# Attention units in pairs of heads: half-array matmuls in place of padded copies

## Chip, cores and metric

The kernel runs on one core of one Trainium2 chip. The metric is the device time of one execution in microseconds. The engines are named TensorE (PE), VectorE (DVE), ScalarE (ACT), GpSimd (POOL) and SyncE (SP).

## What is computed

Two layers of a hybrid decoder over 256 positions and a model width of 1024. Each layer projects the normalised input once (`w_in`), runs three groups of heads side by side, joins them by one output projection (`w_out`), and then a squared-ReLU MLP. The part that matters here is the attention of groups A and C:

```python
# group C: 8 heads of 64 in 2 kv groups of 4, three branches, gates by sigmoid
s_s = einsum('bqghd,bqgtd->bqght', qrb, ks) * scale      # selected blocks (here: all causal keys)
o_s = einsum('bqght,bqgtd->bqghd', softmax(s_s), vs)
s_w = einsum('bqghd,bsgd->bqghs', qrb, kw) * scale       # sliding window (here: all causal keys)
o_w = einsum('bqghs,bsgd->bqghd', softmax(s_w), vw)
o = gb[..., 0:1] * o_c + gb[..., 1:2] * o_s + gb[..., 2:3] * o_w
# group A: 4 heads of 64, keys limited to the top 64 of an indexer's scores
```

Group C's 16 score matrices (8 heads, 2 branches) and group A's 4 are 256x256, causal, fp32. The compressed branch `o_c`, the S5 group B with its GELU and gated unit, and the indexer's top-64 selection run in between.

## The kernel before

All engines run hand-written programs side by side, one per engine, each strictly in its written order, with semaphores (`Signal`: `x.by(instruction)` counts up, `wait_ge(x.sem, x.at(L, n))` waits). fp32 weights come as 92 pieces per layer through a ring of four `raw` buffers: SyncE loads (`piece`), ScalarE makes the high part (`hi`), VectorE or GpSimd the low part (`lo`, `lo_out`), TensorE multiplies three products (`mm3`). Plain fp32 matmuls (`mm`) show in the trace as two passes of load and matmul each.

A causal score matrix of one head is held as 384 columns: 128 queries by 128 keys, and 128 queries by 256 keys. The loop of a layer goes over 20 units, `units`: for each block `b` of heads (2b, 2b+1) of group C its head and branch, then the 4 heads of group A. The stages of unit `i`, by engine:

- TensorE: two score matmuls into bank `pb[i % 2]`, with zero-padded keys (`kT`, `akT`: 128 rows, 64 of them zero, by `mhalf`), after `s_sb` of unit i-2; then three transposes of unit i-3 (after `pn_sb`, banks `pb[2 + u % 2]`); then two value matmuls of unit i-4 (after `pT_sb`) with zero-padded values (`vpad`, `av`: 64 of 128 columns zero); then what `between` names.
- VectorE: after `s_ps`, two evacuations with scale, mask and row maximum (line 1437, `s_sb`); then for unit i-1, after `e_sb`, `reciprocal` and the gate's product (lines 1449, 1452, `cf_sb`); then `between`: rounds of `top8_of_rest`, group C's small works (`c_open1`, `c_gelu`, `c_keys`, `c_max`, `c_probs`), group B's (`y_cube`, `y_gelu`, `y_half`, `y_glu`), `a_mask`, and `h_rest`.
- ScalarE: after `s_sb`, two exponentials with row sums (lines 998, 1000, `e_sb`); then the copy of the transposes of unit i-3 out of PSUM (line 1007, `pT_sb`); then `transposed`, `hi` (pieces 20 to 23), tanh and copies for the other groups, at the end the splits of the outputs.
- GpSimd: after `cf_sb`, the products of exponentials and coefficients (line 748, `pn_sb`), and after units 3, 7, 11, 15 the low part of pieces 20 to 23 (line 738, `lo_out`).

Ahead of the loop TensorE does `s5_kernel`; in `between` it does `c_first` and `a_keys` behind unit 1, `a_queries` behind 4, `c_second` and `s5_out` behind 5 (these wait for ScalarE's copy of the queries, `transposed(7)`, in unit 5), `c_scores` behind 8, `c_transpose` and `y_turned` behind 13, `glu` and `c_values` behind 15. `y_turned` waits for eight transfers (`ytok`) that SyncE issues once VectorE's `y_gelu` is done. The loop ends with `sums_of`, and the output projection follows.

At the start VectorE sets `av` and `vpad` to zero (line 1196), between the low parts of pieces 3 and 4, while GpSimd runs `prep`; GpSimd's `rstd` behind it gates the first tile's copy.

## Time and profile before

| | |
|---|---|
| median of 3 runs | 733.24 us (731.89 to 733.95) |
| profiled execution | 735.1 us, span 733.1 us |
| mean granted clock | 0.967 |
| TensorE busy | 664.8 us (91%), weight loads 586.9 us |
| VectorE, ScalarE, GpSimd busy | 450.8, 367.1, 228.2 us |

The profile is of one execution. Its time stands 2.0 us above its span, and 1.9 us above the median of the other runs. Busy shares are averages over stages with different limits; the two attention loops, from 96 to 166 us and from 447 to 515 us, are under a fifth of the span. PEclk is the granted clock of TensorE, 1.00 for 2.4 GHz and 0.50 for 1.2 GHz.

### The profile page before, as it was taken

How to read it: one execution, taken by the hardware profiler on the slowest of the kernel's cores; microseconds unless marked ns; L12 is line 12 of the kernel's file. 1: busy time of each engine (PE TensorE's matmuls, PEld its weight loads, DVE VectorE, ACT ScalarE, POOL GpSimd, SP SyncE). 2: the span in 40 equal slices, each digit the busy share in tenths (PEclk: the TensorE clock that was granted, in tenths of full speed). 3: DMA queues.
4: the chain of work that ended last, by engine and by line, in shares of the span. 5: the costliest groups of instructions: out<-in, count | busy, mean ns of one | idle time of the engine just before them, and what ended most of it. 6: DMA issues, size and time to landing. Idle time of an engine off the chain costs nothing.

```text
span 733.1 us, 11482 instructions
## 1 busy us (share of the span) xinstructions
PE 664.8 (91%) x4308; PEld 586.9 (80%) x4308; DVE 450.8 (61%) x860; ACT 367.1 (50%) x680; POOL 228.2 (31%) x379
## 2 busy tenths in 40 slices
PE   5959878779899999999999987977989999999996
PEld 4847767568798899988978886756879889999884
DVE  8675974843755559596555659584375555455553
ACT  5542755563544543445545567556354444444542
POOL 5899433441034399980000001544100000000001
PEclk9988998998999999999999999999899999999998
DMA  9485020200685555637535722020065665666541
GB/s 267 125 220 149 30 41 30 73 30 29 202 237 201 170 186 169 225 119 247 168 119 164 228 79 41 30 73 30 29 202 178 196 188 171 208 182 198 177 140 57
DMA packets 62965, 102.77 MB, mean 140 GB/s; under 512 B 20677, under 2 KB 27022, under 8 KB 62878
## 3 DMA queue, kind: packets, MB, share of 16 engines
q1 hardware_dynamic: 58862, 98.63, 44.1%
q0 software_dynamic: 592, 1.70, 0.9%
q10 hardware_dynamic: 3456, 1.70, 0.9%
q8 instruction: 34, 0.56, 0.3%
q14 instruction: 21, 0.17, 0.1%
HBM read 99.66 MB, written 1.31 MB: 138 GB/s over the span
## 4 chain that ended last, share of the span: by engine, by line
PE 72%; DVE 14%; ACT 6%; issue 3%; DMA 2%; POOL 1%; SPq 0%; DVEq 0%; POOLq 0%; ACTq 0%
PE pb L1542 70%; DVE w_lo L1179 5%; DMA raw<-in_w_in 2%; DVE tab_zone L1437 2%; DVE x L1109 1%; ACT w_hi L804 1%; DVE dtmp L1102 1%; ACT tab_zone L1000 1%; PE pb L1675 1%; DVE h_lo L1109 1%; ACT ptmp L1007 1%; DVE cprob L1102 1%; PE pb L1825 1%; POOL sp L584 1%; ACT tab_zone L998 1%
## 5 line engine op out<-in xcount | busy, mean ns | idle before, releaser
L1179 DVE TENSOR_TENSOR w_lo<-raw,w_hi 128x1024 fp32r<-128x1024 f32 (+2 forms) x176 | 225.3, 1298 | 157.3 <-ACT w_hi L804 157.2
L804 ACT ACTIVATE w_hi<-raw 128x1024 fp32r<-128x1024 f32 (+2 forms) x184 | 187.7, 1026 | 224.4 <-PE pb L1542 200.4
L1542 PE MATMUL pb<-h_hi,w_hi 128*128 128x256 f32 x512 | 145.2, 284 | 2.5 <-DVE h_lo L1109 1.8
L1542 PE MATMUL pb<-h_hi,w_lo 128*128 128x256 f32 x512 | 144.9, 283 | 0.0
L1542 PE MATMUL pb<-h_lo,w_hi 128*128 128x256 f32 x512 | 144.9, 283 | 0.0
L1542 PEld LDWEIGHTS pb<-h_hi,w_hi 128*128 128x128 f32 x512 | 98.2, 192 | 4.1 <-DVE w_lo L1179 3.0
L1542 PE MATMUL pb<-w_hi,z_hi 128*128 128x512 f32 x256 | 99.9, 390 | 0.4 <-DVE w_lo L1179 0.4
L1542 PE MATMUL pb<-w_hi,z_lo 128*128 128x512 f32 x256 | 99.8, 390 | 0.0
L1542 PE MATMUL pb<-w_lo,z_hi 128*128 128x512 f32 x256 | 99.6, 389 | 0.0
L1542 PEld LDWEIGHTS pb<-h_hi,w_lo 128*128 128x128 f32 x512 | 98.2, 192 | 0.4
L1542 PE MATMUL pb<-w_hi,h_hi 128*128 128x512 f32 (+2 forms) x224 | 85.8, 383 | 13.9 <-DVE w_lo L1179 10.8
L1542 PEld LDWEIGHTS pb<-h_lo,w_hi 128*128 128x128 f32 x512 | 98.2, 192 | 0.0
L1542 PE MATMUL pb<-w_hi,h_lo 128*128 128x512 f32 (+2 forms) x224 | 83.8, 374 | 0.0
L1542 PE MATMUL pb<-w_lo,h_hi 128*128 128x512 f32 (+2 forms) x224 | 83.8, 374 | 0.0
L748 POOL TENSOR_TENSOR dtmp<-tab_zone,cf 128x128 f32<-128x128 f32 x80 | 40.7, 530 | 124.3 <-PE pb L1542 62.0
L1542 PEld LDWEIGHTS pb<-w_hi,h_hi 128*128 128x128 f32 x224 | 44.0, 196 | 22.2 <-issue 10.7
L1542 PEld LDWEIGHTS pb<-w_hi,z_hi 128*128 128x128 f32 x256 | 48.1, 188 | 10.5 <-DVE w_lo L1179 0.9
L1542 PEld LDWEIGHTS pb<-w_lo,z_hi 128*128 128x128 f32 x256 | 48.1, 188 | 10.1
L1542 PEld LDWEIGHTS pb<-w_hi,z_lo 128*128 128x128 f32 x256 | 48.1, 188 | 9.4
L584 POOL TENSOR_TENSOR tail<-tail 128x1 f32<-128x1 f32 x2 | 0.4, 193 | 177.2 <-ACT proj L1090 177.2
L1542 PEld LDWEIGHTS pb<-w_hi,h_lo 128*128 128x128 f32 x224 | 44.1, 197 | 6.5
L1542 PEld LDWEIGHTS pb<-w_lo,h_hi 128*128 128x128 f32 x224 | 43.6, 195 | 7.0
(304 smaller groups left out, 982.4 us busy)
## 6 DMA issues: line engine op xcount, KB each, us to landing
raw<-in_w_up SPq DMA_DIRECT2D x64, 512.0 KB, 3.7
raw<-in_w_down SPq DMA_DIRECT2D x64, 512.0 KB, 4.3
raw<-in_w_in SPq DMA_DIRECT2D x24, 512.0 KB, 4.7
raw<-in_w_out SPq DMA_DIRECT2D x16, 512.0 KB, 3.8
raw<-in_w_in SPq DMA_DIRECT2D x8, 308.0 KB, 3.5
raw<-in_w_in SPq DMA_DIRECT2D x8, 280.0 KB, 3.3
x<-in_x ACTq DMA_DIRECT2D x4, 256.0 KB, 4.2
u_zone<-proj SPq DMA_DIRECT2D x16, 32.0 KB, 2.1
```

The lines of the kernel that those rows point to most:

```text
L584: step(pool.tensor_tensor(o, a, b, op), wait)
L748: m = pool.tensor_tensor(pn[:, u % 3, a:b], ex[:, u % 3, a:b], cf[:, u % 2, t:t + 1].to_broadcast([PART, b - a]), ALU.mult)
L804: hi_made.by(act.activation(w_hi[:, n % RING, 0:width(n)], raw[:, n % RING, 0:width(n)], ACT.Copy))
L998: step(act.activation(ex[:, i % 3, 0:PART], sc[:, i % 2, 0:PART], ACT.Exp, scale=-1.0, bias=nmx[:, i % 2, 0:1], accum_out=sm[:, i % 3, 0:1 ...
L1000: e_sb.by(act.activation(ex[:, i % 3, PART:384], sc[:, i % 2, PART:384], ACT.Exp, scale=-1.0, bias=nmx[:, i % 2, 1:2], accum_out=sm[:, i % ...
L1007: pT_sb.by(act.activation(pT[:, u % 2, :], pb[2 + u % 2][:, 0:384], ACT.Copy))
L1102: step(dve.tensor_tensor(o, a, b, op), wait)
L1109: return dve.scalar_tensor_tensor(out=o, in0=a, scalar=s, in1=b, op0=op0, op1=op1)
L1179: lo_made.by(dve.tensor_tensor(w_lo[:, n % RING, 0:width(n)], raw[:, n % RING, 0:width(n)], w_hi[:, n % RING, 0:width(n)].bitcast(F32), AL ...
L1437: m = dve.tensor_tensor_reduce(sc[:, i % 2, a:b], pb[i % 2][:, a:b], mask[:, a:b], -(HD ** -0.5), 3e38, ALU.add, ALU.min, nmx[:, i % 2, t: ...
L1542: return pe.matmul(o, l, r, start=start, stop=stop, skip_group_check=True)
L1675: m = pe.transpose(pb[QK_BANK[i]][:, b * SEQ + t * PART:b * SEQ + (t + 1) * PART], src[:, t], ident[:])
```

## The change

The unit of the loop becomes a pair: two heads of one branch. For group C these are head j of kv group 0 and head j of kv group 1 (before, heads 2b and 2b+1 of the same group), since their queries lie on rows 0 to 63 and 64 to 127 of one tile. Scores use row halves of the array (keys unpadded, one half each), the two heads in banks `pb[0]` and `pb[1]`; value products use column halves of the array, with `proj` and a smaller `av` read as they are. `vpad`, its copies, the masks on the key copies and two memsets go. Group C's output now comes in the order (j, g), so its gains and the rows of `w_out` are loaded in that order, by two DMAs in place of one for `gain_c` and for four pieces a layer. There are 10 pairs a layer, each stage handles both heads under one semaphore, the banks for the scores are not doubled any more (the next scores wait for `s_sb` of the pair before), transposes are two pairs behind and values three, and `between` is laid out anew on each engine.

```diff
+TWO_LOADS = (P_IN + 1, P_IN + 2, P_IN + 4, P_IN + 5)
+def landed(n):
+
+    return 16 * sum(2 if i in TWO_LOADS else 1 for i in range(n % RING, n + 1, RING))
...
-        akT = a_zone[:, 0:4 * SEQ].rearrange("p (a t) -> p a t", a=4)
+        akT = a_zone[:, 0:2 * SEQ].rearrange("p (a t) -> p a t", a=2)
...
-        kT = u_zone[:, 4 * SEQ:8 * SEQ].rearrange("p (b g t) -> p b g t", b=2, g=C_KV)
+        kT = u_zone[:, 4 * SEQ:6 * SEQ].rearrange("p (b t) -> p b t", b=2)
...
-        av = sb("av", [PART, TT, A_HEADS, PART])
-        vpad = sb("vpad", [PART, TT, 2, C_KV, 192])
+        av = sb("av", [PART, TT, A_HEADS, HD])
...
-        UNITS = 2 * C_HEADS + A_HEADS
+        UNITS = C_HEADS + A_HEADS // 2
...
-        units = []
-        for b in range(4):
-            for h in (2 * b, 2 * b + 1):
-                for br in range(2):
-                    units.append(("C", h, br, b))
-        for h in range(A_HEADS):
-            units.append(("A", h, 0, h // 2))
+        pairs = [("C", br, b) for b in range(4) for br in range(2)] + [("A", 0, b) for b in range(2)]
+        C_PAIRS = C_HEADS
...
+            for g in range(C_KV):
+                sp.dma_start(vrow_b[4:8, :, HD * g:HD * g + HD],
+                             gain_c.rearrange("l (g j d) -> g j l d", g=C_KV, d=HD)[g]).then_inc(rows_b.sem, 16)
+            for r, src in ((0, gain_a), (2, gain_b), (8, kv_norm_g), (9, s5_glu_b)):
...
+                        dst = raw[:, n % RING, :].rearrange("p (k n) -> p k n", k=2)
+                        if q < 2:
+                            piece(n, dst, wo_l[:, 2 * q:2 * q + 2, half * 512:half * 512 + 512])
+                        else:
+                            for g in range(C_KV):
+                                piece(n, dst[HD * g:HD * g + HD], wo_c[:, g, 2 * q - 4:2 * q - 2, half * 512:half * 512 + 512])
...
+                for p in range(UNITS):
+                    pool.wait_ge(cf_sb.sem, cf_sb.at(L, p + 1))
+                    if p >= 2:
+                        pool.wait_ge(pT_ps.sem, pT_ps.at(L, p - 1))
+                    for m in range(2):
+                        i = 2 * (p % 2) + m
+                        for t, (a, b) in enumerate(((0, PART), (PART, 384))):
+                            w = pool.tensor_tensor(pn[:, i, a:b], ex[:, i, a:b],
+                                                   cf[:, i, t:t + 1].to_broadcast([PART, b - a]), ALU.mult)
+                            if (m, t) != (1, 1):
+                                step(w, False)
+                    pn_sb.by(w)
+                    if p in (1, 3, 5, 7):
+                        lo_out(20 + p // 2)
...
+                for p in range(UNITS + 2):
+                    if p < UNITS:
+                        act.wait_ge(s_sb.sem, s_sb.at(L, p + 1))
+                        if p >= 2:
+                            act.wait_ge(pn_sb.sem, pn_sb.at(L, p - 1))
+                        for m in range(2):
+                            i = 2 * (p % 2) + m
+                            for t, (a, b) in enumerate(((0, PART), (PART, 384))):
+                                w = act.activation(ex[:, i, a:b], sc[:, i, a:b], ACT.Exp, scale=-1.0,
+                                                   bias=nmx[:, i, t:t + 1], accum_out=sm[:, i, t:t + 1])
+                                if (m, t) != (1, 1):
+                                    step(w, False)
+                        e_sb.by(w)
+                    if p >= 2:
+                        v = p - 2
+                        act.wait_ge(pT_ps.sem, pT_ps.at(L, v + 1))
+                        if v >= 2:
+                            act.wait_ge(pv_done.sem, pv_done.at(L, v - 1))
+                        for m in range(2):
+                            w = act.activation(pT[:, 2 * (v % 2) + m, :], pb[2 + m][:, 0:384], ACT.Copy)
+                            if m == 0:
+                                step(w, False)
+                        pT_sb.by(w)
+                    if p in (1, 2):
+                        transposed(6 + p - 1)
+                    if p in (1, 2, 4, 6):
+                        hi(L, 20 + (1, 2, 4, 6).index(p))
+                    if p == 1:
+                        act.wait_ge(tanh_in.sem, tanh_in.at(L, 1))
+                        tanh_c.by(act.activation(gt[:, 2, :], gt[:, 1, :], ACT.Tanh, scale=GELU_A))
+                    if p == 3:
                         act.wait_ge(y_ps.sem, y_ps.at(L, 1))
                         y_sq.by(act.activation(yt, pb[7][:], ACT.Square, scale=0.044715 ** 0.5))
+                    if p == 4:
                         act.wait_ge(y_in.sem, y_in.at(L, 1))
                         y_th.by(act.activation(y2, y2, ACT.Tanh, scale=GELU_A))
+                    if p == 5:
+                        act.wait_ge(cs_max.sem, cs_max.at(L, 1))
+                        cs_exp.by(act.activation(pc2[:], pc2[:], ACT.Exp))
+                    if p == 7:
                         act.wait_ge(yk_ps.sem, yk_ps.at(L, 1))
                         yk_sb.by(act.activation(yg, pb[7][:], ACT.Copy))
+                        act.wait_ge(pcT_ps.sem, pcT_ps.at(L, 1))
+                        pcT_sb.by(act.activation(pcT[:], pb[4][:, 0:SEQ], ACT.Copy))
...
+                    if p == 9:
...
+                    if p == 10:
+                        act.wait_ge(pv_done.sem, pv_done.at(L, C_PAIRS))
...
-                    for t in (av, vpad):
-                        step(dve.memset(t[:], 0.0), False)
...
+                    by_block = [cs[:, i, :].rearrange("p (t j g) -> p t j g", t=TT, g=2) for i in (1, 2)]
+                    tt(by_block[0], by_block[1], gate[:].rearrange("p t (g j n) -> p n t j g", g=2, n=3)[:, 0], ALU.mult)
                     tt(p2, p2, cs[:, 1, :].unsqueeze(2).to_broadcast([PART, 16, 16]), ALU.mult)
-                    for t in range(TT):
-                        m = dve.tensor_tensor(pc[:, t].rearrange("p (g j) n -> p j g n", g=2),
-                                              pc2[:, t].rearrange("p (j g) n -> p j g n", g=2),
-                                              cone[:, t, :].unsqueeze(1).unsqueeze(1).to_broadcast([PART, 4, 2, 16]), ALU.mult)
-                        if t == 0:
-                            step(m, False)
-                    pc_made.by(m)
+                    pc_made.by(dve.tensor_tensor(pc, pc2, cone[:].unsqueeze(2).to_broadcast([PART, TT, C_HEADS, 16]),
+                                                 ALU.mult))
...
+                top = top8_of_rest
+                between = {0: (top, top), 1: (c_open1, top), 2: (c_gelu, top), 3: (top, y_cube, c_keys),
+                           4: (top, y_gelu), 5: (c_max, top), 6: (c_probs, top), 7: (a_mask, y_half), 8: (y_glu,),
+                           9: (lambda: h_rest(8, gm[:, L], out_rows, K_ORDER, 0, 4),),
+                           10: (lambda: h_rest(8, gm[:, L], out_rows, K_ORDER, 4, 2),)}
+                assert sum(w.count(top) for w in between.values()) * 8 == TOPK
+                for p in range(UNITS + 1):
+                    if p < UNITS:
+                        mask = cmask if pairs[p][0] == "C" else abias
+                        dve.wait_ge(s_ps.sem, s_ps.at(L, p + 1))
+                        if p >= 2:
+                            dve.wait_ge(e_sb.sem, e_sb.at(L, p - 1))
                         dve.nop(nofuse=True)
+                        for m in range(2):
+                            i = 2 * (p % 2) + m
+                            for t, (a, b) in enumerate(((0, PART), (PART, 384))):
+                                w = dve.tensor_tensor_reduce(sc[:, i, a:b], pb[m][:, a:b], mask[:, a:b],
+                                                             -(HD ** -0.5), 3e38, ALU.add, ALU.min,
+                                                             nmx[:, i, t:t + 1])
+                                if (m, t) != (1, 1):
+                                    step(w, False)
+                        s_sb.by(w)
+                    if p >= 1:
+                        v = p - 1
+                        kind, br, b = pairs[v]
+                        both = slice(2 * (v % 2), 2 * (v % 2) + 2)
+                        dve.wait_ge(e_sb.sem, e_sb.at(L, v + 1))
+                        if v >= 2:
+                            dve.wait_ge(pn_sb.sem, pn_sb.at(L, v - 1))
+                        w = dve.reciprocal(cf[:, both], sm[:, both])
                         if kind == "C":
+                            step(w)
+                            w = dve.tensor_tensor(cf[:, both], cf[:, both], gate[:].rearrange("p t (g j n) -> p n j g t", g=2, n=3)
+                                                  [:, 1 + br, b], ALU.mult)
+                        cf_sb.by(w)
...
+                between = {0: (c_first, a_keys), 1: (a_queries,), 2: (c_second, s5_out), 4: (c_scores,),
+                           6: (y_turned,), 7: (c_transpose, glu), 8: (c_values,)}
+                for p in range(UNITS + 3):
+                    if p < UNITS:
+                        kind, br, b = pairs[p]
+                        if p >= 1:
+                            pe.wait_ge(s_sb.sem, s_sb.at(L, p))
+                        q, k = (cqrT[:, b], kT[:, br]) if kind == "C" else (aqT[:, b], akT[:, b])
+                        for t, (a, n) in enumerate(((0, PART), (PART, SEQ))):
+                            for m in range(2):
+                                d = slice(HD * m, HD * m + HD)
+                                w = mm(pb[m][:, a:a + n], q[d, t * PART:(t + 1) * PART], k[d, 0:n], t == 0, True)
+                        s_ps.by(w)
+                    if 2 <= p < UNITS + 2:
+                        v = p - 2
+                        pe.wait_ge(pn_sb.sem, pn_sb.at(L, v + 1))
+                        if v >= 1:
+                            pe.wait_ge(pT_sb.sem, pT_sb.at(L, v))
+                        for m in range(2):
+                            for c in range(3):
+                                w = pe.transpose(pb[2 + m][:, c * PART:(c + 1) * PART],
+                                                 pn[:, 2 * (v % 2) + m, c * PART:(c + 1) * PART], ident[:])
+                        pT_ps.by(w)
+                    if p >= 3:
+                        v = p - 3
+                        kind, br, b = pairs[v]
+                        pe.wait_ge(pT_sb.sem, pT_sb.at(L, v + 1))
                         if kind == "C":
                             o = pb[5 + b // 2][:, (b % 2) * SEQ:(b % 2 + 1) * SEQ]
+                            col = (O_VS, O_VW)[br]
+                            vs = [[proj[:, t, col + HD * m:col + HD * m + HD] for m in range(2)] for t in range(TT)]
                         else:
                             o = pb[4][:, b * SEQ:(b + 1) * SEQ]
+                            vs = [[av[:, t, 2 * b + m, :] for m in range(2)] for t in range(TT)]
+                        last = (kind == "A" or b > 2) and br == (kind == "C")
+                        for t in range(TT):
+                            for m in range(2):
+                                w = mm(o[HD * m:HD * m + HD, t * PART:SEQ], vs[t][m],
+                                       pT[:, 2 * (v % 2) + m, t * SEQ:SEQ + t * PART],
+                                       t == 0 and v in (0, C_PAIRS // 2, C_PAIRS), t == 1 and last)
+                        pv_done.by(w)
```

The `between` of before, for comparison: on VectorE `{0: top8, 1: top8, 2: c_open1, 3: top8, 4: c_gelu, 5: top8, 6: top8, 7: (y_cube, c_keys), 9: (y_gelu, c_max, top8), 10: top8, 11: top8, 12: c_probs, 13: a_mask, 15: y_half, 17: y_glu, 19: h_rest, 20: h_rest}`, counted in units, of which two make a pair.

## Rows read from the trace of the kernel before

**Rows 1.** The page of the profile: span, and the chain that ended last by engine.

```profile
span 733.1 us, 11482 instructions
...
PE 72%; DVE 14%; ACT 6%; issue 3%; DMA 2%; POOL 1%; SPq 0%; DVEq 0%; POOLq 0%; ACTq 0%
```

**Rows 2.** Windows, the loops of both layers: busy us (instructions) by engine, granted clock, DMA.

```profile
core 0: us, PE busy (x) PEld busy (x) DVE busy (x) ACT busy (x) POOL busy (x), PEclk, DMA share, GB/s
...
96.00:166.40 70.40, 56.17 (x422) 48.16 (x423) 42.14 (x202) 39.39 (x127) 29.57 (x44) 0.90 0.17 45
...
447.00:514.60 67.60, 54.20 (x423) 46.00 (x423) 42.44 (x202) 39.38 (x127) 29.57 (x44) 0.92 0.18 47
```

**Rows 3.** Timeline, layer 0, unit 11: start us, us, engine, line, instruction.

```profile
133.21 0.28 DVE L1437 CUSTOM_DVE_ANT_0 tab_zone<-pb,cmask 128x128 f32<-128x128 f32 x1
...
133.76 0.16 DVE L1449 RECIPROCAL cf<-sm 128x2 f32<-128x2 f32 x1
...
133.88 0.40 ACT L998 ACTIVATE tab_zone<-tab_zone,nmx 128x128 f32<-128x128 f32 x1 [0.85 <-DVE nmx L1437]
...
134.03 0.62 DVE L1330 MAX8 top<-dtmp 128x8 f32<-128x128 f32 x2
...
134.19 0.97 POOL L748 TENSOR_TENSOR dtmp<-tab_zone,cf 128x128 f32<-128x128 f32 x2 [1.24 <-DVE cf L1452]
...
134.77 0.47 ACT L1007 ACTIVATE ptmp<-pb 128x384 f32<-128x384 f32 x1
...
135.42 0.28 DVE L1437 CUSTOM_DVE_ANT_0 tab_zone<-pb,cmask 128x128 f32<-128x128 f32 x1
```

**Rows 4.** Timeline, layer 0, `y_cube` and the scores after `c_keys`.

```profile
122.08 0.68 DVE L1109 SCALAR_TENSOR_TENSOR yz<-yz,pb 128x512 f32<-128x512 f32 x1
...
123.37 0.28 DVE L1437 CUSTOM_DVE_ANT_0 tab_zone<-pb,cmask 128x128 f32<-128x128 f32 x1
```

**Rows 5.** Timeline, TensorE: scores of one unit, the last sums, and column quarters in layer 1.

```profile
125.77 0.53 PEld L1542 LDWEIGHTS pb<-u_zone 128*128 128x128 f32 x4
...
126.87 0.29 DVE L1437 CUSTOM_DVE_ANT_0 tab_zone<-pb,cmask 128x128 f32<-128x128 f32 x1 [2.59 <-PE pb L1542]
...
166.36 2.98 PEld L1542 LDWEIGHTS pb<-inv,proj 128*128 128x128 f32 x24
...
464.23 1.93 PE L1542 MATMUL pb<-ca,ez 128*32 128x128 f32 x64
...
466.09 0.92 PE L1542 MATMUL pb<-u_zone 128*128 128x128 f32 x4
```

**Rows 6.** Timeline, TensorE: `c_first`, `c_second` and the scores behind `s5_out`, both layers.

```profile
96.07 3.92 PE L1542 MATMUL pb<-dtmp,w 128*64 128x32 f32 x64 [0.85 <-DVE dtmp L1319]
...
112.95 0.38 PE L1542 MATMUL pb<-gk,w2d 64*128 64x32 f32 x2 [1.46 <-ACT w_zone L948]
...
117.93 0.52 PEld L1542 LDWEIGHTS pb<-u_zone 128*128 128x128 f32 x4 [0.20 <-issue]
...
462.78 0.38 PE L1542 MATMUL pb<-gk,w2d 64*128 64x32 f32 x2 [0.92 <-ACT w_zone L948]
...
514.62 2.96 PE L1542 MATMUL pb<-inv,proj 128*128 128x1 f32 x24
```

**Rows 7.** Windows: the end of `s5_out` in layer 0 (columns as in rows 2).

```profile
114.50:117.50 3.00, 3.00 (x64) 3.00 (x60) 0.00 (x0) 0.00 (x0) 0.00 (x0) 0.50 0.02 5
```

**Rows 8.** Timeline, layer 0: `y_glu` on VectorE beside the low part on GpSimd.

```profile
152.60 2.35 POOL L738 TENSOR_TENSOR w_lo<-raw,w_hi 128x1024 fp32r<-128x1024 f32 x1
...
153.54 1.96 DVE L1109 SCALAR_TENSOR_TENSOR dtmp<-yz 128x512 f32<-128x512 f32 x1 [0.51 <-ACT yz L1027]
```

**Rows 9.** Timeline: SyncE's queue, the issues of the S5 output's turn.

```profile
128.41 5.91 SPq L538 DMA_DIRECT2D ytok<-uu  x8
```

**Rows 10.** Timeline, start of the kernel: GpSimd's `prep`, VectorE's memset and low part.

```profile
19.52 2.18 POOL L584 TENSOR_TENSOR sp<-sp,vcol 128x8 f32<-128x8 f32 x2
...
19.65 1.34 DVE L1196 MEMSET vpad<- 128x1536 f32 x1 [0.27 <-issue]
...
20.91 0.74 DVE L1179 TENSOR_TENSOR w_lo<-raw,w_hi 128x616 fp32r<-128x616 f32 x1
```

More of the change, by code:

```diff
@@ L948, in transposed @@
                         m = act.activation(aqT.rearrange("p a b -> p (a b)"), src[:], ACT.Copy)
-                    else:
-                        for g in range(2):
-                            dst = kT[:, :, g, :] if what == 5 else akT[:, g::2, :]
-                            m = act.activation(dst, src[:].rearrange("p (b n) -> p b n", b=2), ACT.Copy,
-                                               scale=mhalf[:, g:g + 1])
-                            if g == 0:
-                                step(m, False)
+                    elif what == 5:
+                        m = act.activation(kT.rearrange("p b t -> p (b t)"), src[:], ACT.Copy)
+                    else:
+                        m = act.activation(akT.rearrange("p a b -> p (a b)"), src[:], ACT.Copy)
                     qk_sb.by(m)
@@ L1025, in _ @@
+                    if p == 8:
                         act.wait_ge(glu_ps.sem, glu_ps.at(L, 1))
@@ L1419, in _ @@
                 s5_lags()
-                between = {0: (top8_of_rest,), 1: (top8_of_rest,), 2: (c_open1,), 3: (top8_of_rest,),
-                           4: (c_gelu,), 5: (top8_of_rest,), 6: (top8_of_rest,), 7: (y_cube, c_keys),
-                           9: (y_gelu, c_max, top8_of_rest), 10: (top8_of_rest,), 11: (top8_of_rest,),
-                           12: (c_probs,), 13: (a_mask,), 15: (y_half,), 17: (y_glu,),
-                           19: (lambda: h_rest(8, gm[:, L], out_rows, K_ORDER, 0, 4),),
-                           UNITS: (lambda: h_rest(8, gm[:, L], out_rows, K_ORDER, 4, 2),)}
@@ L1807, in c_values @@
                     c_open.by(m)
-                between = {1: (c_first, a_keys), 4: (a_queries,), 5: (c_second, s5_out), 8: (c_scores,),
-                           13: (c_transpose, y_turned), 15: (glu, c_values)}
-                for i in range(UNITS + 4):
-                    if i < UNITS:
-                        kind, h, br, _ = units[i]
-                        if i >= 2:
-                            pe.wait_ge(s_sb.sem, s_sb.at(L, i - 1))
-                        q, k = (cqrT[:, h % 4, :], kT[:, br, h // 4, :]) if kind == "C" else (aqT[:, h // 2, :], akT[:, h, :])
-                        mm(pb[i % 2][:, 0:PART], q[:, 0:PART], k[:, 0:PART], True, True)
-                        s_ps.by(mm(pb[i % 2][:, PART:384], q[:, PART:SEQ], k[:, 0:SEQ], False, True))
-                    if 3 <= i < UNITS + 3:
-                        u = i - 3
-                        pe.wait_ge(pn_sb.sem, pn_sb.at(L, u + 1))
-                        if u >= 2:
-                            pe.wait_ge(pT_sb.sem, pT_sb.at(L, u - 1))
-                        for c in range(3):
-                            m = pe.transpose(pb[2 + u % 2][:, c * PART:(c + 1) * PART],
-                                             pn[:, u % 3, c * PART:(c + 1) * PART], ident[:])
-                        pT_ps.by(m)
-                    if i >= 4:
-                        u = i - 4
-                        kind, h, br, b = units[u]
-                        pe.wait_ge(pT_sb.sem, pT_sb.at(L, u + 1))
@@ L1840, in _ @@
-                        mm(o, vs[0], pT[:, u % 2, 0:SEQ], u in (0, C_HEADS, 2 * C_HEADS), False)
-                        pv_done.by(mm(o[:, PART:SEQ], vs[1], pT[:, u % 2, SEQ:384], False,
-                                      (kind == "A" or b > 2) and h % 2 == 1 and br == (kind == "C")))
-                    for work in between.get(i, ()):
+                            vs = [[av[:, t, 2 * b + m, :] for m in range(2)] for t in range(TT)]
+                        last = (kind == "A" or b > 2) and br == (kind == "C")
@@ L1844, in _ @@
+                        for t in range(TT):
[4 more added lines that the diff above has]
+                        pv_done.by(w)
+                    for work in between.get(p, ()):
                         work()
```

121 lines of the change are left out of this document (18 added, 103 removed).

## The prediction, made before the result

> **What bounds the kernel now.** I read four views. The page says that TensorE ends the chain for 72% of the 733.1 us span [rows 1], which invites "fewer TensorE passes, less time". The windows over the two attention loops, 70.4 and 67.6 us, show otherwise there: no engine is busy throughout, TensorE 56 and 54 us, VectorE 42, ScalarE 39, GpSimd 30 [rows 2]. The loops are bound by turns that go round the engines. The timeline gives the price of one turn, and the rows around `c_first`, `c_second` and `s5_out` show where TensorE itself stands and waits for one.
>
> In steady state a unit goes: scores, 1.10 us from the first weight load to VectorE's start [rows 5]; then 0.67 to the first exponential and 0.89 to the copy of the transposes (133.21, 133.88, 134.77) [rows 3]. I call scores-evacuation, exponential and copy a turn. For one unit it takes 0.67 + 0.89 + 0.4 = 1.95 us. Behind the loop TensorE is dense again, so a shift of the loop's end shifts the end of the kernel.
>
> **Prices of a pair.** ScalarE and VectorE do the same instructions on the same shapes, two units in a row, and the semaphore comes after the second. Evacuation: 0.67 plus another 0.55 (133.21 to 133.76) = 1.22. Exponentials 2 x 0.89 = 1.78. Copies 0.8. A turn H is 3.8 us in place of 1.95. VectorE's own stream is 1.1 + 0.28 = 1.38 a pair (133.21 to 134.03 is 0.82 for a unit, of which 0.27 now falls once for two), and a round of top-8 is 1.39 (134.03 to 135.42). GpSimd's products are 2 x 0.97 = 1.94 [rows 3].
>
> Scores S on row halves: no row shows two row halves at once. Below, it costs what one unit does, 1.10; above, serial, 1.10 + 0.65 (the second unit's passes) = 1.75. Column quarters do overlap at fp32: 64 passes of 128 columns take 1.93 us, 30 ns each, and the full-array scores start at once behind them (466.09 against 464.23 + 1.93) [rows 5], so I charge 0.1 us for a change of tiling. But a load of 128 columns cannot shrink: 24 of them with one-column matmuls take 2.98 us, 124 ns each [rows 5]. A pair needs eight, 0.95 us, then the last pass and the latency: S = 1.5. Values have 64-column loads and overlap by column: 0.65 a pair; six transposes 0.65.
>
> The Trainium skill is on both sides here. TensorEngine Tiling (Array Packing), section Theoretical Speedup, gives up to twofold when the contraction is at most 64; by that S would be near 1.10 and is the second rival. TensorE: Matmul & The Clock Gate, section LDWEIGHTS, says a load's time follows its columns, not its rows; by that S stays near 1.5. The load rows bear out the second.
>
> **One layer, turn by turn.** The places where TensorE or VectorE waits for a turn in the new order, each with the work that it then does. The small works between pairs are read like `y_cube` and `c_keys`, 1.29 us (122.08 to 123.37) [rows 4]: `c_open1` 1.45, `c_gelu` 0.7, `c_max` 1.3, `c_probs` 2.2 among GpSimd's products.
>
> To `c_second`: `c_first` 3.9 and `a_keys` 0.3 stay in front [rows 6]. Then S 1.5, evacuation and `c_open1` and `a_queries` 3.25, S 1.5, H and the copy of queries 4.4: 14.85 us. Before it was 112.95 - 96.07 = 16.9 in layer 0 and about 15.7 in layer 1 [rows 2, 6]. The gain is 2.0 and 0.8.
>
> `s5_out` and its start: 117.93 - 112.95 = 5.0 in layer 0, where the granted clock fell to 0.50 [rows 6, 7], and 3.3 in layer 1 (462.78 to 466.09), at full clock [rows 5, 6]. In the new order TensorE idles some 4 us just before, as it did before the low stretch; I take 4.6 in both: gain 0.4, loss 1.3.
>
> From the scores behind `s5_out` to the last sums, in order: S 1.5; pair 3, H + square 0.6 + `y_cube`, `c_keys` 1.3 = 5.7; pair 4, H + high part 0.95 + tanh 0.65 + `y_gelu` 0.6 = 6.0, because `y_gelu` now stands in the same iteration as its tanh and VectorE waits; pair 5, 1.38 + `c_max` + top-8 = 4.1; pair 6, 1.38 + `c_probs` + top-8 = 5.0, and 0.7 more, since `y_turned` now comes before the scores of pair 7 and its eight transfers take 5.9 us to issue from `y_gelu` on [rows 9], some 2 to land, then turn and S; pair 7, H + 0.6 + `glu` 2.4 (1.7 at full clock, 3.4 at half) + S = 8.3; pair 8, `y_glu` is ready after H + 0.8 but GpSimd's `w_lo` lies beside it as before, when a 0.7 us instruction took 1.96 until `w_lo` was over [rows 8]: 6.5. Pair 9 and the tail: H, the splits with `h_rest` 3.7, which delay the last coefficients, GpSimd 0.25 + 1.94, then transposes, copies and values 2.35, and 0.85 for the half clock in part of it, as at the end before: 12.9. Sum 50.7, against 166.36 - 117.93 = 48.4 in layer 0 and the same 48.4 in layer 1.
>
> A layer is 14.85 + 4.6 + 50.7 = 70.15: against 70.3 in layer 0 and 67.5 in layer 1, -0.15 and +2.65.
>
> **Outside the loop.** The memsets of `av` and `vpad` go. In layer 0, `w_lo` waits behind the second one, 19.65 to 20.99, and GpSimd's `prep`, which later gates the first tile's copy, gets on only when `w_lo` is done: 2.18 us for two tiny products [rows 10]. Without the memset `w_lo` ends about 1.25 us sooner: gain 1.2. ScalarE's masked key copies, `vpad` and half of the `av` copies go before the loop, some 2 us, but `c_first` waits for VectorE's `cx` and hides it: nothing. If that cover were gone it would be 0.6. `akT` in one copy saves 0.6 in pair 1, off the path. SyncE issues one DMA more for `gain_c` ahead of the fifth piece, hidden by tile 0 on TensorE, and four pieces of `w_out` as two DMAs each; those are in flight during the loop, long before their use, and SyncE waits there for `lo_made` anyway. Its only late follower would be the `ytok` issues, already counted. `c_probs` in two instructions fewer: in the 2.2.
>
> Sum: -0.15 + 2.65 - 1.2 = +1.3 us. The profiled execution took 735.1 (span 733.1), so it becomes 736.4; the median of the three runs shown, 733.24, becomes 734.6. A difference within 0.3% (2.2 us) is not told from no change.
>
> **Rivals.** First, about even, my forecast: TensorE's savings fall where it waits, and doubled turns cost what fewer turns save. 734.6, chance 0.38; its own range 731 to 735.5.
>
> Second, faster: S comes down to 1.10, as one unit, five times on the path (pairs 1, 2, 3, 7, 8): 2.0 us a layer; with the clock full over `s5_out` a further 1.3. From 734.6 that is 4.0 to 6.6 off: 728 to 730.6. For it: column quarters reach full overlap [rows 5]. Against: the loads. It decides from S below about 1.2. Chance 0.26, including any gain over 2.2 us.
>
> Third, slower, and one mechanism: TensorE's clock. It was at half for 3.0 us of `s5_out` [rows 7] and 0.90 and 0.92 over the loops [rows 2]. Turns of 5 to 8 us with 2.3 us of TensorE work a pair leave it idler than units did. With half clock in all five scores on the path (loads and passes twice as long, +1.2 each where it meets them, say three of five), `glu` (+1.0) and the tail (+0.8) a layer loses 5.4 at most and 2 to 3 as a mean: 738.6 to 740.6; the border of 2.2 us is crossed with half a microsecond more a layer than I charged. For it: each low stretch stands behind an idle one. Chance 0.33 with its lesser forms.
>
> Fourth, the halves don't overlap at all, and the change gives only its regrouping: S = 1.75, five times in two layers +2.5: 737.1. Chance 0.03. The Trainium skill, TensorEngine Tiling (Array Packing), section Key Properties, has each change of tiling mode drain the engine, which speaks against three changes a pair; the scores that start as the column quarters end [rows 5] show no such price, so its sum would be the forecast's with 0.1 us of S already charged.
>
> Slower thus has 0.36, faster 0.26, same 0.38. The range reaches from clock full everywhere with S at 1.3 (-5) to S serial with some more half clock (+5.5): 729.5 to 740.
>
> **What would show it.** In the new profile: the step from the scores' first load to VectorE 1.5 us; 1.2 and 1.8 to exponential and copy; `c_second` 14.9 us after `c_first`; VectorE idle about 2.5 us before `y_gelu`; TensorE waiting for `ytok`'s transfers before pair 7; TensorE busy some 10 us less a loop while the loops stay near 70 us; GpSimd's `prep` 1.2 us sooner. I am wrong if VectorE or ScalarE streams without these stops, so that a loop takes 60 us, or if low clock stretches make it 74.

## The result, and the profile after

The changed kernel takes 745.06 us, median of 4 runs (742.62 to 751.44), beside 733.6 for the kernel before on the same chip: ratio 1.016, 95% interval 1.0112 to 1.0208, clear of no change. It is slower by 11.5 us, outside the range of the prediction (729.5 to 740); the forecast of 734.6 was wrong. The profiled execution took 744.2 (span 742.1), against 735.1 (733.1). The page, its span and its chain [rows 1]:

```profile
span 742.1 us, 11323 instructions
...
PE 63%; DVE 16%; issue 7%; POOL 5%; ACT 4%; DMA 3%; SPq 2%; DVEq 0%; POOLq 0%; ACTq 0%
```

TensorE has lost share of the chain, VectorE and GpSimd have gained it. Windows over the same two stretches as before, first pass of `c_first` to the last sums [rows 2]:

```profile
core 0: us, PE busy (x) PEld busy (x) DVE busy (x) ACT busy (x) POOL busy (x), PEclk, DMA share, GB/s
94.70:169.00 74.30, 52.03 (x422) 37.82 (x422) 38.87 (x182) 37.85 (x126) 29.23 (x44) 0.75 0.18 43
449.70:523.50 73.80, 54.63 (x422) 39.80 (x422) 38.89 (x181) 37.84 (x126) 29.20 (x44) 0.72 0.18 43
```

The loops take 74.3 and 73.8 us, where they took 70.4 and 67.6. VectorE has 3 us less work, TensorE 4 less in layer 0 and as much as before in layer 1, though the padded half of its score and value products is gone: the granted clock has fallen from 0.90 and 0.92 to 0.75 and 0.72. TensorE's instructions in time order, the places of [rows 6]:

```profile
94.75 5.43 PE L1545 MATMUL pb<-dtmp,w 128*64 128x32 f32 x64 [1.85 <-DVE dtmp L1327]
100.12 1.12 PE L1678 MATMUL pb<-ident,ak 128*128 128x128 f32 x4
101.17 1.65 PE L1545 MATMUL pb<-u_zone 64*128 64x128 f32 x8
106.07 1.12 PE L1678 MATMUL pb<-ident,proj 128*128 128x128 f32 x4 [3.25 <-DVE gt L1377]
107.11 1.65 PE L1545 MATMUL pb<-u_zone 64*128 64x128 f32 x8
...
113.42 0.38 PE L1545 MATMUL pb<-gk,w2d 64*128 64x32 f32 x2 [3.18 <-ACT w_zone L959]
...
118.34 0.93 PE L1545 MATMUL pb<-u_zone 64*128 64x128 f32 x8
...
169.00 2.84 PE L1545 MATMUL pb<-inv,proj 128*128 128x1 f32 x24
```
```profile
449.70 5.40 PE L1545 MATMUL pb<-dtmp,w 128*64 128x32 f32 x64 [1.37 <-DVE dtmp L1327]
...
468.33 0.38 PE L1545 MATMUL pb<-gk,w2d 64*128 64x32 f32 x2 [3.18 <-ACT w_zone L959]
...
523.53 2.84 PE L1545 MATMUL pb<-inv,proj 128*128 128x1 f32 x24
```

So the 9.0 us of span fall like this. `c_first` starts 1.3 sooner (94.75, was 96.07). The loop of layer 0 takes 74.25 from `c_first` to the sums, was 70.40: +3.85. From there to `c_first` of layer 1, 280.70, was 280.63: nothing. The loop of layer 1 takes 73.83, was 67.52: +6.3. The rest, 218.6, was 218.5. The same 64 matmuls of `c_first` took 3.92 us before, now 5.43 and 5.40; `c_second` follows it by 18.7 us in both layers, was 16.9 and 15.7. The clock over these pieces of layer 0, the idle stretch before `c_first` first (columns as in the windows above):

```profile
92.90:94.75 1.85, 0.01 (x2) 0.00 (x0) 1.85 (x8) 0.00 (x0) 0.00 (x0) 1.00 0.00 0
94.75:101.17 6.42, 6.42 (x69) 6.02 (x69) 4.48 (x24) 1.86 (x8) 0.00 (x0) 0.65 0.23 63
101.17:113.42 12.25, 5.83 (x28) 3.75 (x27) 8.21 (x40) 6.67 (x23) 4.80 (x9) 0.62 0.22 28
113.42:118.34 4.92, 4.92 (x100) 4.38 (x100) 0.00 (x0) 0.80 (x1) 1.38 (x1) 0.65 0.38 102
118.34:169.00 50.66, 34.87 (x232) 23.67 (x228) 26.14 (x117) 28.52 (x95) 23.05 (x35) 0.80 0.14 38
```

A pair at full clock, with all engines, reads as follows (the row that answers to [rows 3] and the scores of [rows 5]):

```profile
118.34 0.52 PEld L1545 LDWEIGHTS pb<-u_zone 64*128 64x128 f32 x8 [0.20 <-issue]
118.34 0.93 PE L1545 MATMUL pb<-u_zone 64*128 64x128 f32 x8
...
119.45 0.29 DVE L1438 CUSTOM_DVE_ANT_0 sc_zone<-pb,cmask 128x128 f32<-128x128 f32 x1 [6.92 <-PE pb L1545]
...
120.69 0.40 ACT L1004 ACTIVATE tab_zone<-sc_zone,nmx 128x128 f32<-128x128 f32 x1 [6.47 <-DVE nmx L1438]
...
121.02 1.90 POOL L759 TENSOR_TENSOR dtmp<-tab_zone,cf 128x128 f32<-128x128 f32 x4 [6.22 <-DVE cf L1454]
...
122.46 0.84 ACT L1015 ACTIVATE ptmp<-pb 128x384 f32<-128x384 f32 x2
```

The scores of a pair reach VectorE 1.11 us after their first load, the exponentials begin 1.24 later, the copies 1.77 after that. The later pairs, with `y_cube`, `y_gelu` and the turn of `ytok` [rows 4, 9]:

```profile
123.81 0.69 DVE L1119 SCALAR_TENSOR_TENSOR yz<-yz,pb 128x512 f32<-128x512 f32 x1 [1.48 <-ACT yz L1028]
...
125.11 0.28 DVE L1438 CUSTOM_DVE_ANT_0 sc_zone<-pb,cmask 128x128 f32<-128x128 f32 x1
...
130.45 0.69 DVE L1119 SCALAR_TENSOR_TENSOR uu<-yz,pb 128x512 f32<-128x512 f32 x1 [2.47 <-ACT yz L1031]
130.93 1.63 SPq L503 DMA_DIRECT2D raw<-in_w_out  x2
...
132.60 5.11 SPq L547 DMA_DIRECT2D ytok<-uu  x8
...
139.22 1.11 PE L1770 MATMUL pb<-ident,ytok 128*128 128x128 f32 x4 [1.19 <-DMA ytok<-uu]
...
142.10 0.29 DVE L1438 CUSTOM_DVE_ANT_0 sc_zone<-pb,cmask 128x128 f32<-128x128 f32 x1 [1.64 <-PE pb L1545]
```

And the start: the low part that began at 20.91 behind the memset of `vpad` [rows 10] now begins at 19.42:

```profile
19.42 1.61 DVE L1189 TENSOR_TENSOR w_lo<-raw,w_hi 128x616 fp32r<-128x616 f32 x2 [1.12 <-ACT w_hi L815]
```

### The profile page after: what moved, and what is told of

Read it like the earlier page. It is cut to its first block, busy times and chain, and to the rows that moved or that the text cites. A ratio compares the mean times of both kernels' runs of the same rounds, so it can differ in the third digit from the quotient of the medians.

```text
span 742.1 us, 11323 instructions
## 1 busy us (share of the span) xinstructions
PE 657.5 (89%) x4308; PEld 567.2 (76%) x4308; DVE 443.1 (60%) x818; ACT 361.3 (49%) x668; POOL 226.1 (30%) x379
## 4 chain that ended last, share of the span: by engine, by line
PE 63%; DVE 16%; issue 7%; POOL 5%; ACT 4%; DMA 3%; SPq 2%; DVEq 0%; POOLq 0%; ACTq 0%
PE pb L1545 62%; DVE w_lo L1189 5%; POOL dtmp L759 2%; DVE dtmp L1112 2%; DMA raw<-in_w_in 2%; DVE x L1119 1%; POOL w_lo L747 1%; ACT tab_zone L1004 1%; SPq L547 1%; DVE sc_zone L1438 1%; ACT w_hi L815 1%; DVE h_lo L1119 1%; DVE cn L1287 1%; DVE dtmp L1327 1%; DMA ytok<-uu 1%
## 5 line engine op out<-in xcount | busy, mean ns | idle before, releaser
L1004 ACT ACTIVATE tab_zone<-sc_zone,nmx 128x128 f32<-128x128 f32 x80 | 35.4, 443 | 69.8 <-DVE nmx L1438 69.8
```

Source lines behind the costliest of these rows:

```text
L1004: w = act.activation(ex[:, i, a:b], sc[:, i, a:b], ACT.Exp, scale=-1.0, bias=nmx[:, i, t:t + 1], accum_out=sm[:, i, t:t + 1])
```

## Experiments

Two theories were set against each other. A: TensorE's clock made the loss; the pieces of the forecast hold at full clock. B: the pairs' turns cost more than charged, and the clock only follows. All times are medians, the ratio is to the kernel before on the same chip, with its 95% interval. That neighbour took 733.6 us beside the changed kernel, 734.4 beside e1 to e4, 734.0 beside e5 to e8 and 734.1 beside e10 to e13; what a run gains or loses is told against its own neighbour.

| kernel | us | ratio | span, clock of the profile |
|---|---|---|---|
| changed | 745.1 | 1.016 (1.0112 to 1.0208) | 742.1, 0.931 |
| e1 changed, filled at the start | 738.1 | 1.0055 (1.0028 to 1.0082) | 736.2, 0.946 |
| e2 changed, filled | 732.6 | 0.9972 (0.9946 to 0.9998) | 730.0, 0.981 |
| e3 before, filled | 727.3 | 0.9902 (0.9864 to 0.994) | 725.5, 0.981 |
| e4 pairs, whole array | 750.7 | 1.0229 (1.0183 to 1.0274) | 751.4, 0.948 |
| e5 single heads, half forms | 754.7 | 1.0274 (1.0239 to 1.031) | 755.8, 0.925 |
| e6 changed, ytok first | 745.6 | 1.015 (1.0123 to 1.0177) | 745.3, 0.926 |
| e7 before, memsets first | 732.6 | 0.9985 (0.9958 to 1.0011) | 730.5, 0.969 |
| e8 changed, filled (7 more in the tail), ytok first | 734.4 | 0.9994 (0.9969 to 1.0018) | 729.2, 0.983 |
| e10 single heads, half scores | 741.6 | 1.0108 (1.0083 to 1.0133) | 740.4, 0.946 |
| e11 single heads, half values | 735.1 | 1.0018 (0.9994 to 1.0041) | 735.4, 0.967 |
| e12 pairs, whole array, filled as e8 | 740.2 | 1.0083 (1.0052 to 1.0114) | 735.3, 0.986 |
| e13 before, filled, memsets moved | 724.9 | 0.9892 (0.9866 to 0.9918) | 726.9, 0.983 |

**Filling the waits (e1, e2, e3).** The filling is work that nobody reads, whole-array matmuls of the identity into a bank that is free at that place:

```diff
+            def fill(n, bank=6):
+                for _ in range(n):
+                    mm(pb[bank][:, 384:512], ident[:], ident[:], True, True)
...
                 def c_first():
-                    pe.wait_ge(cx_made.sem, cx_made.at(L, 1))
                     pe.wait_ge(qk_sb.sem, qk_sb.at(L, 5))
+                    fill(8)
+                    pe.wait_ge(cx_made.sem, cx_made.at(L, 1))
...
                 def a_queries():
+                    fill(14)
...
                 def c_second():
+                    fill(14)
```

> The changed kernel with 36 more matmuls a layer of the identity by itself (128 columns, nobody reads them), put where TensorE waits at the start of the loop: 8 before c_first, 14 before the queries' transposes, 14 before c_second. Theory A (the clock made the loss: c_first took 5.4 us instead of 3.9 and the stretch to c_second 18.7 instead of the 14.9 forecast, because TensorE had stood idle and its clock then fell to half): c_first is back at about 3.9, c_second comes 15.0 to 16.0 us after it, each layer loses 3 us, 738 to 740 us. Theory B (the doubled turns themselves make the stretch long, the clock only follows): the granted clock rises but c_second stays 18 us behind c_first and the time stays at 744 to 746.

e2 adds 6, 6, 6 and 4 before the transposes of iterations 4 to 7, 5 after iteration 5, 5 before `y_turned`, and 18 and 10 before the transposes of iterations 10 and 11 (bank 4).

> The same and further such matmuls in the long waits of the later pairs, before the value products of the tail too: the clock should be full nearly everywhere in the loop and over the first passes of the output projection. Theory A: both loops near 66 to 68 us and the time 730 to 734, level with the kernel before or under it. Theory B: both loops stay over 72 us and the time 742 to 747, since the filling can only stand in the way.

e3 does the same in the kernel before, at the five places that its expectation names, 40 matmuls a layer.

> Control: the kernel before, whose own loops had granted clocks of 0.90 and 0.92, with the same kind of filling in its four longest waits a layer (4 matmuls before c_first, 10 before the first value product, 6 before c_second, 9 before the turn of the block probabilities, 11 in the tail). Theory A: it has low stretches of its own to lose, about 1.5 us a layer at s5_out and 1 in the tail, 728 to 731. Theory B: no change, 733 to 734. If the filled change of the run beside it ends above this one, the change loses by its turns as well as by the clock.

TensorE's rows of e1 in both layers, then windows over the loops of e2 and of e3:

```profile
94.54 3.92 PE L1545 MATMUL pb<-dtmp,w 128*64 128x32 f32 x64
...
109.58 0.38 PE L1545 MATMUL pb<-gk,w2d 64*128 64x32 f32 x2 [0.99 <-ACT w_zone L959]
```
```profile
446.75 3.92 PE L1545 MATMUL pb<-dtmp,w 128*64 128x32 f32 x64
...
461.80 0.38 PE L1545 MATMUL pb<-gk,w2d 64*128 64x32 f32 x2 [0.99 <-ACT w_zone L959]
```
```profile
94.00:161.60 67.60, 60.43 (x598) 49.33 (x598) 38.72 (x181) 37.84 (x126) 29.23 (x44) 1.00 0.19 47
444.75:511.47 66.72, 60.44 (x600) 49.33 (x599) 38.21 (x179) 37.84 (x126) 29.25 (x44) 1.00 0.18 48
```
```profile
95.87:161.00 65.13, 59.16 (x495) 51.67 (x495) 42.77 (x201) 39.17 (x127) 29.61 (x44) 0.97 0.19 49
441.90:507.10 65.20, 59.42 (x497) 51.85 (x496) 42.13 (x197) 39.17 (x127) 29.60 (x44) 0.97 0.18 49
```

Theory A holds for the larger part: with 36 filling matmuls a layer the changed kernel loses 3.7 us to the kernel before, where it lost 11.5. `c_first` is back at 3.92, `c_second` comes 15.04 us behind it in both layers (forecast 14.85). In e2 the clock is full throughout the loops, they are 67.6 and 66.7 us, and the kernel gains 1.8. The control gains too, 7.1 us, and its loops are 65.1 and 65.2. So of the 11.5 us, 5.3 remain when both are filled (732.6 against 727.3 on one chip), and the other 6.2 go with the clock: B holds for the 5.3. In the spans, 730.0 and 725.5, that is +2.5 and +1.5 in the loops, 1.9 less before `c_first`, and 2.2 behind the first loop, where e2's output projection begins at half clock (in e3 the granted clock is 1.00 from 160 to 176):

```profile
150.00:162.00 12.00, 10.15 (x89) 8.46 (x88) 3.45 (x14) 8.45 (x27) 3.80 (x8) 1.00 0.12 44
162.00:172.00 10.00, 10.00 (x46) 8.77 (x47) 2.27 (x4) 1.97 (x7) 1.49 (x4) 0.66 0.01 2
```

**Half forms or pairs (e4, e5, e10, e11, e12).** e4 keeps the order of pairs and widens the products; e5 keeps single heads and narrows them, on the padded copies that the kernel before makes anyway; e10 and e11 are the two halves of e5's edit. e4 and e12 leave out the padding as well, so that each head of a pair gets the sum of both heads' products: they stand for the time of whole-array passes only.

```diff
 e4:
-                                w = mm(pb[m][:, a:a + n], q[d, t * PART:(t + 1) * PART], k[d, 0:n], t == 0, True)
+                                w = mm(pb[m][:, a:a + n], q[:, t * PART:(t + 1) * PART], k[:, 0:n], t == 0, True)
 ...
 e5, e10 (d: the head's 64 rows):
-                        mm(pb[i % 2][:, 0:PART], q[:, 0:PART], k[:, 0:PART], True, True)
+                        mm(pb[i % 2][:, 0:PART], q[d, 0:PART], k[d, 0:PART], True, True)
 ...
 e5, e11:
-                            vs = [vpad[:, t, br, h // 4, a:a + PART] for t in range(TT)]
+                            vs = [vpad[:, t, br, h // 4, HD:PART] for t in range(TT)]
 ...
```

> The changed kernel in its order of pairs, but every score and value product over the whole array, as the padded copies had it (here without the padding, so each head of a pair gets the sum of both heads' scores and value products; the time of the passes is that of padded ones). Per pair the scores cost about 0.7 us more and the values 0.8 more at full clock. If the half-array forms are what leaves TensorE too thinly used and lets the clock fall: c_first back at 3.9, loops' clock back at 0.90, and the time 739 to 744 in spite of the longer passes. If the regrouping into pairs does it: c_first stays at 5.4, the clock stays near 0.75 and the longer scores come on top, 748 to 752.

> The kernel before, one head at a time and with its padded copies still made, but its score products read only the 64 rows of the head and its value products only the 64 columns: the half-array forms without pairs, so nothing overlaps. If the half forms by themselves lower the granted clock: the loops fall from 0.90 and 0.92 to about 0.75, c_first takes over 5 us, and the time is 738 to 742. If they cost nothing and the pairs' longer turns are the cause: the loops stay at 68 to 70 us and the time at 732 to 735.

`c_first` of e4 in both layers, then of e5 (with the loads of one unit's scores), and of e10 in layer 0:

```profile
94.80 5.94 PE L1545 MATMUL pb<-dtmp,w 128*64 128x32 f32 x64 [1.47 <-DVE dtmp L1327]
...
455.52 5.04 PE L1545 MATMUL pb<-dtmp,w 128*64 128x32 f32 x64 [0.72 <-DVE dtmp L1327]
```
```profile
97.09 3.92 PE L1542 MATMUL pb<-dtmp,w 128*64 128x32 f32 x64 [0.30 <-DVE dtmp L1319]
...
120.96 0.52 PEld L1542 LDWEIGHTS pb<-u_zone 64*128 64x128 f32 x4 [0.20 <-issue]
```
```profile
96.44 6.02 PE L1542 MATMUL pb<-dtmp,w 128*64 128x32 f32 x64 [0.76 <-DVE dtmp L1319]
```

e4 took 5.94 us for it after 1.47 us idle, with whole-array scores ahead; e5 took 3.92 behind half-array scores, with 0.30 us idle. So half-array scores are not needed for the loss here: the regrouping brings it by itself. The length of the wait does not decide it alone either. In layer 1 of e4 the same passes took 5.04 us behind a wait of 0.72, and in layer 0 of e10, single heads with scores on 64 rows, 6.02 behind 0.76, while the kernel before took 3.92 behind 0.85 [rows 6]. What does show is that filling in front of `c_first` brings the 3.92 back (e1). And e5 is the slowest kernel of all, 754.7 us, outside both of its forecasts, though its `c_first` ran at full clock. Its windows, and a stretch of the kernel before in which most of the same units run:

```profile
121.00:131.00 10.00, 10.00 (x62) 6.83 (x59) 5.72 (x32) 6.03 (x18) 5.22 (x7) 0.99 0.01 2
131.00:156.60 25.60, 25.60 (x76) 14.53 (x74) 16.31 (x71) 11.52 (x39) 9.55 (x15) 0.50 0.19 53
```
```profile
119.67:140.00 20.33, 15.02 (x95) 12.34 (x93) 16.90 (x76) 12.71 (x40) 11.44 (x16) 1.00 0.15 41
```

In e5 the clock fell to half while TensorE was busy for 25.6 of 25.6 us, and it had been busy all of the 10 us ahead. The kernel before stood idle for a quarter of the time and kept the full clock over these 20.3 us. My first reading, a low stretch stands behind an idle one, is half the story: half-array passes did it without an idle moment. The Trainium skill, TensorE: Matmul & The Clock Gate, section What's actually happening, lets the clock go by how busy TensorE has been; by that rule alone this stretch would be at full clock, and the measurement decides otherwise. What the chip counts instead stays open here.

> The kernel before in single heads with only the score products cut to the head's 64 rows (values stay over the whole array). With both forms cut it took 754.7 us, and TensorE's clock was at half for 26 us a layer while TensorE was busy throughout (136 to 156: 20.0 of 20.0 us busy, clock 0.50). If the clock follows how much of the array works and row halves alone suffice: low stretches of over 10 us a layer, 742 to 752. If both forms have to come together: 733 to 736, loops at 0.88 to 0.92.

> The same with only the value products cut to 64 columns (scores whole). If column halves lower the clock as row halves do: 740 to 750. If only rows matter, the columns being the narrower part of the work anyway: 733 to 736.

Row halves cost 7.6 us by themselves, column halves nothing that this run separates from no change (interval 0.9994 to 1.0041). Both together cost 20.7, far more than the sum: at half clock TensorE itself becomes what the loop waits for (the 25.6 us above). Why the two together hold the clock down so long is not shown. The loops of e10:

```profile
96.40:171.10 74.70, 67.80 (x422) 52.80 (x423) 42.16 (x201) 39.22 (x127) 29.61 (x44) 0.77 0.18 43
450.30:521.90 71.60, 63.11 (x422) 49.51 (x423) 42.02 (x201) 39.32 (x127) 29.64 (x44) 0.83 0.18 44
```

> The changed kernel in pairs with score and value products over the whole array (each head of a pair gets the sum of both, as in the fourth run) and the filling of the eighth. If, once the clock is held up, half forms are worth what their passes save (0.65 us a pair for scores, 0.65 for values where they are on the path, some 5 places a layer): 736 to 741, against 732 to 734 for the filled change. If they are worth nothing at full clock because the turns of the other engines set the pace: 731 to 734.

```profile
95.40:166.20 70.80, 67.63 (x613) 63.96 (x613) 38.54 (x180) 37.87 (x126) 29.28 (x44) 1.00 0.18 45
448.40:518.50 70.10, 67.58 (x614) 63.93 (x614) 37.84 (x175) 37.87 (x126) 29.30 (x44) 1.00 0.17 45
```

At full clock pairs over the whole array take 70.8 and 70.1 us a loop, pairs in halves 67.6 and 66.7, single heads over the whole array (e3, clock 0.97) 65.1 and 65.2. The half forms give 3.3 us a layer, the regrouping costs 5.3. In kernel time the half forms give 5.7 us between e12 and e8, which have the same filling. What inside the regrouping costs the 5.3, the turns of double length, the banks for the scores that are no longer doubled, or the new layout of `between`, no run separates. As the kernels run, unfilled, the regrouping costs 16 us (e4) and the half forms give back some 5 in pairs, while in single heads, where nothing overlaps, they cost 20.7.

**The queue and the memsets (e6, e7, e8).** e6 changes one line, `if n == 26:` to `if n == 25:` in front of the eight `ytok` issues; e8 makes that change in e2 and raises the filling of iteration 11 from 10 to 17; e7 moves the two memsets to VectorE's first instructions.

> The changed kernel with one line moved: SyncE issues the eight ytok transfers before the piece of w_out that is now two transfers, not behind it. ytok's issues begin about 0.8 to 1.6 us sooner and y_turned stops waiting (it waited 1.2 us in layer 0 and 2.8 in layer 1). If that queue is on the path: 742 to 743.5. If VectorE's probabilities and top-8 would have held pair 7 back anyway: no change, 744 to 745.5.

> The kernel before with its two memsets of the padded copies moved to VectorE's first instructions, nothing else: the only part of the change that I booked as a gain outside the loop. If the memset behind which w_lo and with it GpSimd's preparation waited is what brought c_first 1.3 us forward (94.75 against 96.07): c_first at about 94.8 and 732 to 732.7. If the shorter copies of ScalarE brought it: c_first stays at 96.1 and the time at 733.6.

> The changed kernel with the filling of the second run, 7 more of those matmuls behind the value products of pair 7 in the tail (there TensorE had idled 1.5 us and the output projection's first passes ran at half clock, 163 to 170), and ytok's transfers first. If clock and queue explain what is left but the turns: 2 us for the clock and 1 to 2 for the queue, 728.5 to 730.5. The filled kernel before took 727.3; what stays above that is the price of the doubled turns. If the turns of pairs are the larger part: 731 to 733.

e6 in order of time, `y_gelu` on VectorE, the issues, the turn on TensorE:

```profile
132.16 0.69 DVE L1119 SCALAR_TENSOR_TENSOR uu<-yz,pb 128x512 f32<-128x512 f32 x1 [2.47 <-ACT yz L1031]
...
132.88 5.50 SPq L547 DMA_DIRECT2D ytok<-uu  x8
...
140.71 0.65 PE L1770 MATMUL pb<-ident,ytok 128*128 128x128 f32 x4 [0.97 <-DMA ytok<-uu]
```

SyncE takes the issues up 0.03 us after the end of `y_gelu` (132.85), where it took 1.46 (131.14 to 132.60). VectorE's start on pair 7 comes 5.53 us after that on pair 6 (136.88 to 142.41), was 6.94, in layer 1 5.82, was 6.04; before it VectorE now waits 0.23 and 0.51 us, so the rest is its own work. So the queue was on the path, by 1.4 and 0.2 us, and the kernel's time shows nothing of it (ratio 1.015, was 1.016): the scores behind `s5_out`, which the edit can't touch, reach VectorE at 121.16 instead of 119.45 in this execution. Half clock for a little longer or shorter is worth as much as the queue; that this is what hid it is my reading, not shown. e8, at 734.4 above both of its forecasts, is not better than e2 either (729.5 to 736.5 against 729.3 to 736.1), though in its profiled execution the clock behind the first loop is 0.95 (162 to 166) and 0.75 (166 to 172), where e2 has 0.68 and 0.65. e7: TensorE's next wait for a low part ended 20.85 us after its first pass, was 22.19; but that first pass came 0.9 later (13.46, was 12.59), since the memsets now stood ahead of it; `c_first` at 95.91, was 96.07. The time decides nothing (interval 0.9958 to 1.0011).

**The best kernel (e13).** e3 with nine more filling matmuls, and the memsets behind the low parts of pieces 16 and 17:

```diff
                 for n in range(12, 20):
                     lo(n)
+                    if L == 0 and n in (16, 17):
+                        step(dve.memset((av, vpad)[n - 16][:], 0.0), False)
```

> The filled kernel before (727.3) with 9 more filling matmuls before the value product of the eighth unit, where its clock still fell (128 to 134), and the two memsets of the padded copies moved behind the low parts of pieces 16 and 17, where VectorE waits 1.9 us a piece. If the memset's place is worth the 1.3 us by which the gate of the second tile moved: 724.5 to 726. If moving them only shifts the wait, as the kernel with the memsets first gave 0.5 us: 726.5 to 727.5.

It beats both kernels, 1.1% under the one before (median 724.9; the profiled execution took 729.0). That it beats e3 is not shown (their intervals overlap). The first passes of tile 1 came 1.3 us sooner (55.18, was 56.48), but `cx` only 0.5 (its memset at 93.30, was 93.80): between the two VectorE waited for ScalarE's copies.

## Why the prediction was wrong, point by point

**The step that failed** is the sum of a layer, 14.85 + 4.6 + 50.7 = 70.15, and what it was set against. I made it at full clock but for 0.85 us in the tail, put the clock's further cost at nothing, and left it to the third rival with 0.33 and "2 to 3 as a mean" a layer. Filling turns a loss of 11.5 us into a gain of 1.8, 13.3 us; the kernel before had 7.1 of the same to lose, so by the clock the change added 6.2, or 3.1 a layer. That is close to the rival's own price: the mechanism was named and roughly sized, and booked at nothing. The other 5.3 us are there with both kernels filled, where I had +1.3 in all. I had put the clock's cost in scores, `glu` and the tail; it began in `c_first` (1.5 us each layer), whose cover of dense work I took for granted: I had TensorE's work before it shrink and never asked how long TensorE would then wait for `cx`. It is done with the first scores at 92.9 and idle for 1.85 us, where it was 0.85 [rows 6]; in layer 1 it is 1.37, where there was none. That wait goes with the slow passes in the changed kernel, but its length alone does not explain them, as e4 and e10 show. And I looked for idleness alone, where half-array passes lower the clock with none (e5).

**To `c_second`, 14.85:** right at full clock (15.04), 18.7 as run. **S, 1.5** (a pair's scores, first load to VectorE): too high. 1.11 at full clock, about 1.8 at half. I argued that loads of 128 columns can't shrink; eight loads of 64 rows took 0.52 us in the row above, no more than four of 128 rows in [rows 5]. Four loads of 64 rows with no partner took 0.52 as well (e5, 120.96): it is the side-by-side that saves, not the fewer rows. The Trainium skill's factor of up to two (TensorEngine Tiling (Array Packing), section Theoretical Speedup) is what the trace shows, loads included. The second rival's mechanism was there, and its gain was eaten by the clock and the regrouping. **Turns:** 1.24 and 1.77, predicted 1.2 and 1.8. **`s5_out` 4.6:** 4.92 in layer 0, part of it at half clock. **From there to the sums, 50.7:** 50.66 in layer 0. That is two errors that cancel, S too dear and the clock too full: pair 7 came 6.94 after pair 6 (5.7), pair 8 7.41 (8.3). In e2, at full clock, the whole loop took 67.6 and 66.7 where I had 70.15. **VectorE idle before `y_gelu`:** 2.47, predicted 2.5. **TensorE waiting for `ytok`:** 1.2 and 2.8 us. I had called the two-part pieces hidden, and any cost to `ytok` counted; their issues (130.93) stood in front of `ytok`'s (132.60). It cost pair 7 1.4 and 0.2 us (e6), too little to be seen in the kernel's time.

**TensorE busy 10 us less a loop:** no, 4 and none, since at half clock the passes that are left take longer. **Memsets, -1.2:** `c_first` came 1.3 sooner, but e13 suggests that the memsets alone give 0.5 and ScalarE's shorter copies, which I booked at nothing, the rest; this is argued from two rows, not shown. **The forecast of +1.3** is also too low without the clock: both kernels filled, it is +5.3 (e2 against e3), and with e8 in place of e2 +7.5, each against its own neighbour. In the profiled executions of e2 and e3 2.2 of it stand behind the first loop, at half clock. I set my 70.15 against loops of the kernel before, 70.3 and 67.5, that held half-clock time of their own; at full clock those are 65.1 and 65.2 (e3), so the regrouping costs more than it seemed to. I had named 74 us a loop as what would make me wrong, and it was 74.3 and 73.8.

## What to carry to other kernels

Before a change that makes TensorE's work shorter or narrower in a stage bound by turns between engines, read the granted clock of that stage, then ask of each dense group what TensorE does ahead of it in the new order: here 3.9 us of work took 5.4 where TensorE came to wait 1 us longer ahead of it, and what followed took longer too. The length of the wait is no safe measure (5.0 and 6.0 us in e4 and e10 behind shorter ones); filling the wait is the test. Half-array forms need their partner beside them (some 5 us gained in pairs, 20.7 lost in single heads), and the regrouping that brings the partner has its own price: 5.3 us a layer at full clock for 3.3 given back. Where TensorE must wait, work that nobody reads, sized to the wait, is a cheap test of the clock: it took 7.1 us off the tuned kernel.

## What was not expected of the hardware

The clock stood at 0.50 for 25.6 us in which TensorE was busy throughout, with products over 64 rows or 64 columns and whole-array transposes between them (e5). Products cut to 64 rows cost 7.6 us, products cut to 64 columns nothing measurable. Two row halves share their loads' time: eight loads of 64 rows in 0.52 us, as long as four without a partner. And the kernel before, with most of its half-clock stretches gone, is 7.1 us faster with 40 matmuls a layer more.
